# Seven of eleven chunk pairs of the up matrix by seven quarter products instead of eight, in a two-block network on one core

## The reference

```python
def conv_gated_ffn(x, w_up, w_gate, conv_w, conv_b, w_down):
    u = x @ w_up                                          # 512x1024 @ 1024x2816
    g = causal_dwconv(x @ w_gate, conv_w, conv_b)         # the same shape, then 3 taps over the tokens
    return (jax.nn.silu(g) * u) @ w_down                  # 512x2816 @ 2816x1024

# in each of the two layers of the first network:
x = layer_norm(DN_ALPHA * x + mix, ln_mix_g[i], ln_mix_b[i])
ffn = conv_gated_ffn(x, ...)
ple = jax.nn.sigmoid(x @ ple_w_gate[i]) * (p[i] @ ple_w_proj[i])
x = layer_norm(DN_ALPHA * x + ffn + ple, ln_ffn_g[i], ln_ffn_b[i])
```

## Time and profile before

| what | value |
|---|---|
| device time, three runs | 1748.43, 1748.67, 1748.83 us (median 1748.67) |
| span of the profiled execution | 1747.5 us, 22538 instructions |
| matmul time of TensorE | 1736.9 us, 99% of the span, 9213 matmuls |
| VectorE busy, ScalarE busy, GpSimd busy | 61%, 48%, 1% |
| read from memory, written to it | 149.78 MB, 2.10 MB |
| first `up` chunks to the end of `down`, first block | about 250 to 610 us |
| the same of the second block | about 900 to 1290 us |

### The profile page before, as it was taken

The page is one execution under the profiler, slowest core; times in us unless marked ns, Lnnn a source line. Parts: engine busy times, 40 slices in busy tenths (PEclk is TensorE's granted clock), DMA queues, the critical chain, the costliest instruction groups (busy, mean ns, idle before and its releaser), DMA issues.

```text
span 1747.5 us, 22538 instructions
## 1 busy us (share of the span) xinstructions
PE 1736.9 (99%) x9213; PEld 1409.7 (81%) x9213; DVE 1063.6 (61%) x1666; ACT 847.1 (48%) x1330; POOL 18.4 (1%) x21
## 2 busy tenths in 40 slices
PE   9999999999999999999999999999999999999999
PEld 7887988888888897777778888888898866778766
DVE  6788864444433465877784444443378866656674
ACT  7789643333332355666463333342255455534542
POOL 0000100000000000000200000000000000000000
PEclk9999999999999999999999999999999999999999
DMA  5331232222222321111132232323213221132111
GB/s 216 110 121 45 89 109 97 97 97 97 97 97 96 97 85 61 62 58 51 61 112 96 96 98 95 101 90 109 97 61 107 96 70 63 61 97 97 61 60 49
DMA packets 44678, 155.43 MB, mean 89 GB/s; under 512 B 5280, under 2 KB 5536, under 8 KB 44576
## 3 DMA queue, kind: packets, MB, share of 16 engines
q1 hardware_dynamic: 44576, 153.99, 26.6%
HBM read 149.78 MB, written 2.10 MB: 87 GB/s over the span
## 4 chain that ended last, share of the span: by engine, by line
PE 90%; ACT 4%; DVE 4%; issue 1%; DMA 1%; SPq 0%; DVEq 0%; ACTq 0%
PE bank L553 89%; ACT tmp L1316 2%; DVE tmp L1990 1%; DVE wl L1999 1%; DMA wraw<-in_wstream 1%; ACT taps L1316 1%; ACT wh L1316 1%; PE bank L1261 0%; DVE XL L1999 0%; DVE sbl L1999 0%; ACT HL L1316 0%; DVE HL L1999 0%; ACT Y L1316 0%; DVE X L1987 0%; DVE acc_q L1987 0%
## 5 line engine op out<-in xcount | busy, mean ns | idle before, releaser
L553 PE MATMUL bank<-XH,wh 128*128 128x512 f32 (+1 forms) x1504 | 583.4, 388 | 3.7 <-ACT wh L1316 1.1
L553 PE MATMUL bank<-XL,wh 128*128 128x512 f32 (+1 forms) x1504 | 573.5, 382 | 0.0
L553 PE MATMUL bank<-XH,wl 128*128 128x512 f32 (+1 forms) x1504 | 573.5, 382 | 0.0
L1999 DVE TENSOR_TENSOR wl<-wraw,wh 128x1024 fp32r<-128x1024 f32 (+1 forms) x264 | 319.6, 1220 | 237.8 <-ACT wh L1316 237.2
L1316 ACT ACTIVATE wh<-wraw 128x1024 fp32r<-128x1024 f32 (+1 forms) x264 | 276.2, 1052 | 250.4 <-PE bank L553 242.7
L553 PEld LDWEIGHTS bank<-XH,wh 128*128 128x128 f32 x1504 | 282.8, 188 | 68.7 <-issue 9.3
L553 PEld LDWEIGHTS bank<-XH,wl 128*128 128x128 f32 x1504 | 282.8, 188 | 55.2
L553 PEld LDWEIGHTS bank<-XL,wh 128*128 128x128 f32 x1504 | 283.0, 188 | 52.3 <-issue 0.7
L1987 DVE SCALAR_TENSOR_TENSOR tmp<-bank,prm,tmp 128x511 f32<-128x511 f32 x88 | 65.9, 749 | 172.1 <-ACT tmp L1316 170.6
L553 PE MATMUL bank<-HH,wh 128*128 128x512 f32 (+1 forms) x420 | 155.7, 371 | 0.0
L553 PE MATMUL bank<-HH,wl 128*128 128x512 f32 (+1 forms) x420 | 154.1, 367 | 0.0
(11 more groups left out here) (350 smaller groups left out, 2181.9 us busy)
## 6 DMA issues: line engine op xcount, KB each, us to landing
wraw<-in_wstream SPq DMA_DIRECT2D x276, 512.0 KB, 3.5
out<-X SPq DMA_DIRECT2D x8, 256.0 KB, 2.3
X<-in_xt SPq DMA_DIRECT2D x3, 512.0 KB, 8.9
pts<-in_pt SPq DMA_DIRECT2D x4, 256.0 KB, 3.7
eb<-lab SPq DMA_DIRECT2D x16, 64.0 KB, 2.0
cst<-in_consts SPq DMA_DIRECT2D x1, 810.5 KB, 10.1
X<-in_xt SPq DMA_DIRECT2D x2, 256.0 KB, 4.2
wraw<-in_wstream SPq DMA_DIRECT2D x2, 256.0 KB, 4.8
```

The source lines that it names most:

```text
L553: return pe.e.matmul(o, l, r, start=start, stop=stop, skip_group_check=True)
L1999: return dve.e.tensor_tensor(o, x, h.bitcast(F32), ALU.subtract)
```

## The change

The weights of `up` and the input are each cut into quarters: the contraction into channels 0 to 511 and 512 to 1023 (blocks k = 0 to 3 and 4 to 7), the tokens into 0 to 255 (`lo`) and 256 to 511 (`hi`), the output columns into the even and the odd chunk of a pair f, f + 1. The product of a pair, which took 16 blocks of 512 columns, is now made of seven products of four blocks with 256 columns each, 28 in all. Three of the seven use plain weights, four use sums of weight quarters (`tw`); four use sums of input quarters (`XS`), three plain input. This is done for the first 14 chunks (`PAIRS = 7`) of both layers; the last 8 are as before.

- **TensorE** (`product`): a pair uses banks 0 to 2 or 3 to 5, the two gates banks 6 and 7. Two banks' contents are read by other engines halfway (`u_e` by ScalarE, `u_c` by VectorE), and TensorE waits for `u_c` before it goes on accumulating into the same half bank: once after 20 of the pair's 28 half-width blocks, once before the last four.
- **ScalarE**: two copies of 256 columns out of a bank for each pair, and the cast of four input sums for each layer.
- **VectorE**: five additions or subtractions of 256 columns for each pair, and for each layer four sums of input quarters (128 x 1024 each) and their four remainders.
- **The weight stream**: a pair has 44 blocks instead of 32. Sums of weights are no part of the stream in memory; a unit with such blocks is loaded in two pieces of 256 KB (`pieces`, `landed`), and SyncE waits for the sums (`tw`) before it loads them.
- **The sums of weights** are made in memory: GpSimd issues, for each layer, four copies and four accumulating transfers of 1.84 MB from memory to memory (7 pairs x 128 x 512 x 4 bytes), each after the one before has landed. The first layer's eight start when `w_lo` is 12, the second layer's when it is 24. They stand ahead of the `acc_s` additions in GpSimd's program.
- Semaphores are merged here and there (`prm_out`, `side_in`, `pt_in`), which adds no wait.

```diff
 def ffn_order(layer):
     out = []
-    for f in range(FT):
+    for p in range(PAIRS):
+        f, up, tw, gate = 2 * p, f"up{layer}", f"tw{layer}", f"gate{layer}"
+        out += [(up, k, f) for k in range(KD)] + [(tw, k, p) for k in range(16)] + [(gate, k, f) for k in range(KD)]
+        out += [(up, k, f + 1) for k in range(4, KD)] + [(gate, k, f + 1) for k in range(KD)]
+    while len(out) % NU:
+        out.append(None)
+    for f in range(2 * PAIRS, FT):
         out += [(f"up{layer}", k, f) for k in range(KD)] + [(f"gate{layer}", k, f) for k in range(KD)]
     return out
...
+    def pieces(self, u):
+
+        sums = [(b := self.order[NU * u + 4 * h]) is not None and b[0][:2] == "tw" for h in range(2)]
+        return [(0, NU * 128, False)] if not any(sums) else [(512 * h, 512 * h + 512, sums[h]) for h in range(2)]
+
+    def landed(self, u):
+
+        return 16 * sum(len(self.pieces(v)) for v in range(u % RAW, u + 1, RAW))
...
-        sp.e.dma_start(m.wraw[u % RAW][:, :], a["wstream"][u]).then_inc(s.raw[u % RAW], 16)
+        for c0, c1, summed in w.pieces(u):
+            if summed:
+                mat, k, p = w.order[NU * u + c0 // 128]
+                layer = int(mat[2:])
+                sp.wait_ge(s.tw, TW_STEPS[layer][k // 4])
+                src = a["tw"][k // 4, layer, p]
+            else:
+                src = a["wstream"][u][:, c0:c1]
+            sp.e.dma_start(m.wraw[u % RAW][:, c0:c1], src).then_inc(s.raw[u % RAW], 16)
...
-        for f in range(FT):
+        lo, hi = slice(0, 256), slice(256, 512)
+        A = lambda k, ts: (XH[:, k, ts], XL[:, k, ts])
+        X_S = lambda j: lambda k: (m.XS[layer][j][:, k % 4, lo], m.XS[layer][j][:, k % 4, hi])
+
+        def product(mat, c, k0, o, x, first, last):
+
+            for k in range(k0, k0 + 4):
+                xh, xl = x(k)
+                block(mat, k, c, o, xh, xl, first and k == k0, last and k == k0 + 3)
+
+        for p in range(PAIRS):
+            f, n = 2 * p, 5 * (PAIRS * layer + p)
+            up, tw, gate = f"up{layer}", f"tw{layer}", f"gate{layer}"
+            b = bank[3 * (p % 2):3 * (p % 2) + 3]
+            if p < 2:
+                pe.wait_ge(s.pg_u, 8 * layer + (4, 6)[p])
+            else:
+                pe.wait_ge(s.u_e, 2 * (PAIRS * layer + p - 1))
+                pe.wait_ge(s.u_c, n - 5)
+            product(up, f, 0, b[0][:, lo], lambda k: A(k, lo), True, False)
+            product(up, f, 4, b[0][:, hi], lambda k: A(k, lo), False, True)
+            pe.wait_ge(s.xs_l, 4 * layer + 1)
+            product(tw, p, 0, b[1][:, lo], X_S(0), True, False)
+            pe.wait_ge(s.xs_l, 4 * layer + 3)
+            product(tw, p, 4, b[1][:, hi], X_S(2), False, True)
+            product(tw, p, 8, b[2][:, lo], lambda k: A(k - 4, hi), True, True)
+            pe.wait_ge(s.u_c, n + 1)
+            product(tw, p, 12, b[0][:, lo], X_S(1), False, True)
+            for odd in range(2):
+                if odd:
+                    pe.wait_ge(s.u_c, n + 3)
+                    pe.wait_ge(s.xs_l, 4 * layer + 4)
+                    product(up, f + 1, 4, b[1][:, lo], X_S(3), False, True)
+                if p:
+                    pe.wait_ge(s.f_conv, FT * layer + f + odd - 1)
+                else:
+                    pe.wait_ge(s.pg_u, 8 * layer + 7 + odd)
+                for k in range(KD):
+                    block(gate, k, f + odd, bank[6 + odd][:, :], XH[:, k, :], XL[:, k, :], k == 0, k == KD - 1)
...
+            if f0 == 0:
+                for j in range(4):
+                    act.wait_ge(s.xs_f, 4 * layer + j + 1)
+                    fn(m.XS[layer][j][:, :, 0:256], m.SF[layer][j], ACT.Copy).then_inc(s.xs_h, 1)
...
+                a = bank[3 * (f // 2 % 2)][:, 0:256]
+                feed_group(f"up{layer}", range(KD), [f])
+                act.wait_ge(s.stream, w.done(f"up{layer}", KD - 1, f))
+                fn(sqr[0][:, 0:256], a, ACT.Copy).then_inc(s.u_e, 1)
+                feed_group(f"tw{layer}", range(16), [f // 2])
+                act.wait_ge(s.stream, w.done(f"tw{layer}", 15, f // 2))
+                fn(sqr[1][:, 0:256], a, ACT.Copy).then_inc(s.u_e, 1)
...
+        a11, a21, a12, a22 = (X[:, k0:k0 + 4, ts] for k0 in (0, 4) for ts in (lo, hi))
+        n = dve.mark(tt(xs[0], a21, a22, ALU.subtract))
+        dve.wait_ge(dve.own, n)
+        n = dve.mark(tt(xs[1], xs[0], a11, ALU.subtract))
+        dve.wait_ge(dve.own, n)
+        tt(xs[2], a11, a21, ALU.subtract).then_inc(s.xs_f, 3)
+        tt(xs[3], xs[1], a12, ALU.add).then_inc(s.xs_f, 1)
...
+            if f0 == 0:
+                for j in range(4):
+                    dve.wait_ge(s.xs_h, 4 * layer + j + 1)
+                    less(m.XS[layer][j][:, :, hi], xs[j], m.XS[layer][j][:, :, lo]).then_inc(s.xs_l, 1)
...
+                if f % 2 == 0:
+                    feed_group(up, range(KD), [f])
+                    dve.wait_ge(s.stream, w.done(up, KD - 1, f))
+                    dve.wait_ge(s.u_e, 2 * (PAIRS * layer + p) + 1)
+                    tt(sqr[0][:, lo], sqr[0][:, lo], b[0][:, hi], ALU.add).then_inc(s.u_c, 1)
+                    feed_group(tw, range(16), [p])
+                    dve.wait_ge(s.u_e, 2 * (PAIRS * layer + p) + 2)
+                    tt(sqr[0][:, hi], sqr[1][:, lo], b[1][:, hi], ALU.add).then_inc(s.u_c, 1)
+                    dve.wait_ge(s.u_c, 5 * (PAIRS * layer + p) + 2)
+                    tt(sqr[1][:, hi], b[1][:, lo], sqr[0][:, hi], ALU.subtract).then_inc(s.u_c, 1)
+                    tt(sqr[0][:, hi], sqr[0][:, hi], b[2][:, lo], ALU.add).then_inc(s.u_c, 1)
+                else:
+                    feed_group(up, range(4, KD), [f])
+                    dve.wait_ge(s.stream, w.done(up, KD - 1, f))
+                    tt(sqr[1][:, lo], b[1][:, lo], sqr[1][:, lo], ALU.subtract).then_inc(s.u_c, 1)
+                    dve.wait_ge(s.u_c, 5 * (PAIRS * layer + p) + 5)
...
+    def copy(dst, src, after):
+        pool.wait_ge(s.tw, 16 * after)
+        pool.e.dma_start(dst, src).then_inc(s.tw, 16)
+
+    def add(dst, src, after):
+        pool.wait_ge(s.tw, 16 * after)
+        pool.e.dma_start(dst, src, accum_op=ALU.add, max_dma_last_dim=8192).then_inc(s.tw, 16)
+
+    for layer in range(2):
+        t1, t3, t4, t2 = (a["tw"][t, layer].rearrange("n p c -> (n p) c") for t in range(4))
+        w11, w12, w21, w22 = (a[n][layer].rearrange("n p c -> (n p) c") for n in ("w11", "w12", "w21", "w22"))
+        done = 8 * layer
+        pool.wait_ge(s.w_lo, (12, 24)[layer])
+        copy(t1, w12, done)
+        copy(t3, w12, done + 1)
+        add(t1, w11, done + 2)
+        add(t3, w22, done + 3)
+        copy(t2, t3, done + 4)
+        add(t2, w11, done + 5)
+        copy(t4, t2, done + 6)
+        add(t4, w21, done + 7)
```

More of the change, by code:

```diff
@@ L22 @@
 ALPHA = 4.0 ** 0.25
+PAIRS = 7
+XS0 = 14
 TAPS = 31
@@ L141, in __init__ @@
                 m, k, c = block
-                ends = k == self.depth(m) - 1
+                ends = k == self.depth(m) - 1 or (m[:2] == "tw" and k % 4 == 3)
                 if self.by_token(m, c):
@@ L388, in place @@
                 m.PP.append(sb(same, f"PP{layer}", [128, KD, S]))
+                m.SF.append([x[:, i, :, :] for x in [sb(same, f"SF{layer}", [128, 3, 4, 256])] for i in range(3)])
             m.HH.append(sb(ph, f"HH{layer}", [128, FT, S], FR))
@@ L391, in place @@
                 m.pts.append(sb(same, f"pts{layer}", [128, 2, S]))
+                sb(same, f"between{layer}", [128, 6, S])
+                m.SF[layer].append(sb(same, f"SG{layer}", [128, 4, 256])[:, :, :])
             m.HL.append(sb(ph, f"HL{layer}", [128, FT, S], FR))
@@ L435, in place @@
         m.pick, m.pick2 = sb(ph, "pick", [128, 128], FR), sb(ph, "pick2", [128, 128], FR)
+    m.XS = [[(m.HH, m.HL)[j // 2][layer][:, XS0 + 4 * (j % 2):XS0 + 4 * (j % 2) + 4, :] for j in range(4)] for layer in range(2)]
     m.sba = [[sba[:, c] for _, c, _ in GR], [x[:, 0:c.stop - c.start] for x, (_, c, _) in zip((m.sqr[0], m.acc_q, m.acc_s), GR)]]
@@ L485, in unit @@
     return m.wraw[u % RAW][:, :], m.wh[w.slot[u]][:, :], m.wl[w.slot[u]][:, :]
+TW_STEPS = [[16 * n for n in order] for order in ((3, 4, 8, 6), (11, 12, 16, 14))]
 def sync_program(sp, m, s, w, a):
@@ L504, in pt @@
         for k in range(2):
-            sp.e.dma_start(m.pts[layer][:, k, :], a["pt"][layer][:, k * S:(k + 1) * S]).then_inc(s.pt_in[2 * layer + k], 16)
+            sp.e.dma_start(m.pts[layer][:, k, :], a["pt"][layer][:, k * S:(k + 1) * S]).then_inc(s.pt_in[k], 16)
     x(0, 1, s.x_in[0])
-    first(0, s.first_in)
+    first(0, s.side_in)
     x(1, 1, s.x_in[1])
@@ L712, in ffn @@
+        for f in range(2 * PAIRS, FT):
             bu, bg = bank[(2 + 2 * f) % 6], bank[(3 + 2 * f) % 6]
-            if f < 3:
-                pe.wait_ge(s.pg_u, 8 * layer + 4 + 2 * f)
+            if f < 2 * PAIRS + 3:
+                pe.wait_ge(s.u_e, 2 * PAIRS * (layer + 1))
+                pe.wait_ge(s.u_c, 5 * PAIRS * (layer + 1))
             else:
@@ L1326, in round_to @@
```

(7 more changed lines are left out.)

65 lines of the change are left out of this document (41 added, 24 removed).

## The result

The changed kernel takes 1788.44 us (median of 4 runs, 1787.94 to 1789.41), the kernel before 1748.74 in the same comparison: a ratio of 1.0228, 95% interval 1.0213 to 1.0242. It is 40 us slower. The forecast was 1742, with a range up to 1772, and a chance of 0.36 for slower. The profiled execution has a span of 1787.2 us.

The account below looks back on a forecast made before the run. TensorE was taken to bound the kernel (matmuls in hand for 99% of the span): 1747.5 span - 11.4 for the products + 4.8 for stalls = 1740.9, plus 1.2 from span to median, so 1742 us; range 1737 to 1772.

Parts of the forecast that it names:

- the sixteen transfers: GpSimd's memory-to-memory transfers ahead of the layer norm additions: 6.6 us each, fifteen landed 17 us early, cost taken as 0.
- the second rival: GpSimd's additions come late behind the transfers, and TensorE stands still in the layer norm: 1759 to 1811 us; chance 0.37.
- doubled cost: Accumulating transfers read two sources: 12.2 us each, copies 6.6; additions 17 us late, 1759 us.
- outer bound: Weight stream keeps its 0.30 of the engines: transfers 9.0 and 17.0 us, additions 69 us late, 1811 us.
- the 8.1 us that were allowed: Average time per transfer at which fifteen still land by 182.3 us, when late additions on GpSimd cost nothing.
- the cheapest of the bounds: Every transfer at the queue's plain rate, 6.6 us, in time with 17 us in hand.
- TensorE's own term: Up chunk pairs on TensorE go from 10.88 to 10.06 us, 0.82 less; fourteen pairs: -11.4 us.
- The chain behind a chunk: TensorE waits in the pairs for VectorE's sum: stalls of 0.1 to 0.6 us, 2.4 per layer, +4.8 in all.
- Weight units: Eleven more per layer on ScalarE (1.06 us each) and VectorE (1.22) fit their idle time: nothing, except in the chain.
- input sums: VectorE's four sums and remainders once a layer: taken as 0, 0.3 us to spare, 2 us a layer if it fails.
- The third rival: The sixteen transfers slow the weight stream between 61 and 182 us: +2 to +5, 1744 to 1747 us; chance 0.06.

Follow-up runs that it names:

- no transfers, sum first: Changed kernel without sums of weights (plain quarters loaded), ScalarE's copy and VectorE's sum ahead of the weight unit in each pair: 1737.81 us, ratio 0.9938 against the kernel before.
- the third experiment: Changed kernel with its eight accumulating transfers copying instead of adding, same shapes and order, so the sums are wrong: 1756.11 us, one run.

## Why the prediction was wrong

**The step that failed is that of the sixteen transfers**: a term taken as 0, because a transfer was sized at 6.6 us. It measured 11.1 on average. The mechanism, the due time and its place were right: the second rival is what happened, and its price was between its doubled cost and its outer bound. By its working the additions were due at 182.3 us; the first started at 228.1, 45.8 late. TensorE itself came to the sum 6.7 us later than before (the late load, above all), so that it waited 37.9 and not 44.6. Taken apart by runs:

| from, to | us | what |
|---|---|---|
| before to no transfers, sum first | 1748.6 to 1737.8 | seven products, -10.8 (forecast -11.4) |
| to no transfers | to 1742.5 | stalls of the pair chain, +4.7 |
| to second layer's transfers later | to 1749.6 | contention of the first chain, +7.1 |
| to the changed kernel | to 1788.4 | the chain ahead of the additions, +38.9, of it 37.9 the hole |

**Why the size was off.** I took the queue's rate at full engines and one pass over the bytes, and left out two things that I had priced among the rivals: the second source and the share of the weight stream. Either was enough to break the 8.1 us that were allowed. Beside the stream but without adding, the average was 8.9. Without the stream it would have been about 9.4 by my estimate, from the transfers of the changed kernel that had no weights beside them (copies of 7.3 us, one accumulating transfer of 11.9). With both it was 11.1. The price of each case was worked out in the prediction; what was wrong was to take the one case in which neither holds. The Trainium skill's rule of two source reads (Collectives: The Full Stack, The bandwidth ceiling) agrees with the trace: 1.8 times the engine time of a copy. It was a reason to weigh the late case above the other, since only the cheapest of the bounds was in time.

**TensorE's own term** was right: 0.82 a pair forecast, 0.84 measured. **The chain behind a chunk** came out at 4.7 for the +4.8 forecast, with some luck: an odd pair lost about 0.5 us and not 0.6, and pair 0, for which the forecast had nothing, lost about 0.5 as well (in the kernel without transfers two matmuls start 0.51 us apart there, at 255.93 and 256.44). **Weight units, input sums**: nothing, as said. With the transfers out of the way the forecast of 1742 was met (1742.5).

**The third rival** (slower weight stream) came true beside the second and was priced too low, 2 to 5 us where the first chain cost 7.1; I had taken the cases as alternatives, and they add. Nor did I count the clock, which had fallen to its lower level at the end of the hole.

## What to carry to other kernels

Work that an engine does in order is as late as everything ahead of it: before a chain of transfers goes ahead of other work on a queue, multiply their number by the dearest bound, not the cheapest, and if only the cheapest fits, put the transfers behind the work. DMA engines that look 30% busy do not make a transfer between memory and memory free: here the loads beside it landed after 8.6 us instead of 3.9. So place it where the loads have slack and pause it where they have none. When another engine's small result gates a dense stream of matmuls, do it before the bulk work in that engine's order; here it was worth 4.7 us for a few moved lines.

## What the runs showed of the hardware

- A copy from memory to memory of 1.84 MB landed 6.9 to 9.4 us after its issue in the changed kernel, an accumulating transfer of the same size 11.6 to 17.0. In the same place and shape it was 10.0 against 15.6 from issue to issue.
- How long such a transfer takes follows the weights that move beside it: among the copies of the third experiment 7.5 us with none and 10.0 to 10.6 with 1.05 to 1.49 MB. Alone, an accumulating transfer took 11.9 us (one case).
- From 62 to 226 us, with such transfers in flight, 512 KB of weights landed after 8.6 us instead of 3.9 (medians).
- Matmuls of 256 columns start 119.8 ns apart and of 512 columns 226.7, so that halving the width costs 6%; 28 half-width blocks for 16 whole ones save 7.5% of their time and not 12.5%.
